# Two-block transformer step on one Trainium2 core: each expert weight unit of 1 MB asked for by two transfers of 512 KB

## The reference

```
# router: a group of 4, then the two best of its 8 experts; gates[n, e] is zero elsewhere
for e in range(N_EXPERTS):                               # 32
    hid = jax.nn.silu(t @ w_eg[e]) * (t @ w_eu[e])       # w_eg, w_eu: 1024 x 512
    out = out + gates[:, e:e + 1] * (hid @ w_ed[e])      # w_ed: 512 x 1024
```

## Time and profile before

| | |
|---|---|
| time, median of 3 runs | 1771.27 us |
| the profiled execution | 1775.45 us, its span 1773.4 us |
| granted TensorE clock, mean over the span | 0.995 of full speed |
| PE busy | 1745.6 us, 98% of the span |
| DVE, ACT, POOL busy | 954.2, 725.9, 42.0 us |
| HBM read | 426.70 MB, 241 GB/s over the span |
| `w_ed` units on line 338 | 64 of 1024 KB, median 18.5 us from issue to landing |
| `w_eg`, `w_eu` units into mring | 63 and 62 of 1024 KB, median 14.1 and 16.1 us |

### The profile page before, as it was taken

One profiled execution on the slowest core, in us unless ns is written; L12 is line 12 of the kernel. 1 busy time (PEld: TensorE's weight loads), 2 busy tenths in 40 slices (PEclk: granted clock), 3 DMA queues, 4 the chain that ended last, 5 costly groups with the idle time before them and its releaser, 6 DMA issues.

```text
span 1773.4 us, 24576 instructions
## 1 busy us (share of the span) xinstructions
PE 1745.6 (98%) x9801; PEld 1338.4 (75%) x9801; DVE 954.2 (54%) x1258; ACT 725.9 (41%) x1005; POOL 42.0 (2%) x57
## 2 busy tenths in 40 slices
PE   9999999999999999999999999999999999999998
PEld 8876454444445488888988888878888879888886
DVE  6684111111111286666787666676666864676665
ACT  5562111111111254346566434764346445554444
POOL 3000000000000000000000000000000001200000
PEclk9999999999999999999999999999999999999999
DMA  9278999999999855554435555365555544555552
GB/s 308 96 277 340 395 422 418 417 421 422 422 422 422 343 191 190 192 186 151 143 120 184 190 189 190 131 226 190 189 190 193 190 150 156 180 194 190 191 168 83
DMA packets 191242, 428.81 MB, mean 242 GB/s; under 512 B 7316, under 2 KB 145664, under 8 KB 166592
## 3 DMA queue, kind: packets, MB, share of 16 engines
q1 hardware_dynamic: 187952, 418.41, 64.7%
q0 software_dynamic: 3216, 9.37, 1.5%
HBM read 426.70 MB, written 1.05 MB: 241 GB/s over the span
## 4 chain that ended last, share of the span: by engine, by line
PE 89%; DVE 6%; ACT 3%; issue 1%; DMA 0%; DVEq 0%; ACTq 0%
PE pw L544 64%; PE acc L544 23%; DVE wl L1969 1%; PE pw L933 1%; ACT arena L1732 1%; DVE x L2431 0%; DMA raw<-in_odd_w_in 0%; ACT sm L1548 0%; ACT wh L1387 0%; DVE aa L1987 0%; DVE sm L2696 0%; DVE scr L2693 0%; PE pw L966 0%; PE pw L1315 0%; ACT arena L1710 0%
## 5 line engine op out<-in xcount | busy, mean ns | idle before, releaser
L544 PE MATMUL pw<-aa,wh 128*128 128x512 f32 (+1 forms) x2288 | 520.7, 354 | 0.7 <-ACTq L1800 0.4
L1969 DVE TENSOR_TENSOR wl<-raw,wh 128x2048 fp32r<-128x2048 f32 x204 | 460.9, 2297 | 95.4 <-ACT wh L1387 92.6
L544 PEld LDWEIGHTS pw<-aa,wh 128*128 128x128 f32 x2288 | 395.9, 190 | 54.5 <-issue 3.4
L1387 ACT ACTIVATE wh<-raw 128x2048 fp32r<-128x2048 f32 x204 | 380.0, 1907 | 40.3 <-DMA raw<-in_odd_w_in 23.2
L544 PE MATMUL acc<-wh,aa 128*128 128x512 f32 x1088 | 345.9, 391 | 0.4 <-DVE aa L2230 0.4
L544 PE MATMUL pw<-mring,arena 128*64 128x512 f32 x1512 | 333.9, 594 | 1.4 <-issue 1.3
L544 PE MATMUL pw<-aa,wl 128*128 128x256 f32 x1880 | 324.7, 283 | 0.0
L544 PEld LDWEIGHTS pw<-aa,wl 128*128 128x128 f32 x1880 | 281.4, 191 | 14.0
L544 PEld LDWEIGHTS pw<-mring,arena 128*64 128x64 f32 x1512 | 106.7, 137 | 202.5 <-issue 200.2
L544 PEld LDWEIGHTS acc<-wh,aa 128*128 128x128 f32 x1088 | 204.5, 188 | 43.0 <-DVE wl L1969 0.8
L544 PE MATMUL acc<-wl,aa 128*128 128x512 f32 x544 | 212.2, 390 | 0.0
(11 more groups left out here) (436 smaller groups left out, 1271.4 us busy)
## 6 DMA issues: line engine op xcount, KB each, us to landing
raw<-in_ffn_w_in SPq DMA_DIRECT2D x88, 1024.0 KB, 5.1
mring<-in_w_ed SPq DMA_DIRECT2D x64, 1024.0 KB, 18.5
mring<-in_w_eg SPq DMA_DIRECT2D x63, 1024.0 KB, 14.1
mring<-in_w_eu SPq DMA_DIRECT2D x62, 1024.0 KB, 16.1
raw<-in_ffn_w_out SPq DMA_DIRECT2D x44, 1024.0 KB, 5.0
raw<-in_odd_w_in SPq DMA_DIRECT2D x24, 1024.0 KB, 5.4
raw<-in_w_in SPq DMA_DIRECT2D x12, 1024.0 KB, 9.7
raw<-in_even_w_in SPq DMA_DIRECT2D x11, 1024.0 KB, 5.4
```

The costliest lines, as they stand in the source:

```text
L544: return pe.matmul(out, lhs, rhs, start=start, stop=stop, skip_group_check=True)
L1387: act.activation(wh[:, u % RING, :], raw[:, u % RING, :], ACT.Copy).then_inc(sig(f"{ep}_hi"), 1)
L1969: dve.tensor_tensor(wl[:, u % RING, :], raw[:, u % RING, :], wh[:, u % RING, :].bitcast(F32), ALU.subtract).then_inc(sig(f"{ep}_lo"), 1)
```

## The change

Each unit is now asked for by two transfers, issued one right after the other: the first half of the unit's rows (2 of 4, or 1 of 2, in every partition), then the second half. In a partition that is 4 KB each, one behind the other in HBM and in the slot. Each half adds 16 to the same semaphore as before, and PE waits for 32 where it waited for 16. Slots, order of units, waits of SP and places of PE's waits stay as they were. The two new lines in `expert_unit` move all later line numbers by 2.

```
-                sp.dma_start(dst, src).then_inc(sig(f"{landed}{n}"), 16)
+                rows_ = src.shape[1] // 2
+                for part in (slice(0, rows_), slice(rows_, 2 * rows_)):
+                    sp.dma_start(dst[:, part, :], src[:, part, :]).then_inc(sig(f"{landed}{n}"), 16)
...
                 if n not in held:
-                    pe.wait_ge(sig(f"m_landed{n}"), i * 16 + 16)
+                    pe.wait_ge(sig(f"m_landed{n}"), i * 32 + 32)
                 elif isinstance(i, int):
-                    pe.wait_ge(sig(f"e_landed{n}"), 16)
+                    pe.wait_ge(sig(f"e_landed{n}"), 32)
                 else:
-                    pe.wait_ge(sig(f"m_landed{n}"), i * 16)
+                    pe.wait_ge(sig(f"m_landed{n}"), i * 32)
...
-                pe.wait_ge(sig(f"{'m' if odd else 'e'}_landed{n}"), twos * 16 + 16)
+                pe.wait_ge(sig(f"{'m' if odd else 'e'}_landed{n}"), twos * 32 + 32)
```

## The result

The changed kernel takes 1784.59 us (median of 4 runs, 1783.35 to 1785.37) against 1770.9 us (median of 4 runs of the kernel before): 1.0067 times the time before, 95% interval 1.0055 to 1.0079. It is slower, by 10 to 14 us, and lies above the stated range. The forecast was 1773.5 us.

A forecast was written before the change was run, and what follows sets the result against it. The DMA stream was taken to bound the end of the expert stage. 17 + 3 = 20 ns a unit over 108 units, with 43 earlier ones absorbed, gave +2.2 us on 1771.27: 1773.5 us, range 1770.5 to 1780.5.

The forecast's parts named there:

- What bounds the kernel: Expert stage: PE lives on loads made ahead until used up; the stage ends with the DMA stream, 1.35 us recoverable at most.
- The price of the packets: Expert units as 4 KB instead of 8 KB packets: 17 ns more a unit, 20 ns with completions; ends 0 and 69 ns.
- My high end of 69 ns: Expert units: 8 more packets a unit at a fixed part of 8.6 ns, giving 9.3 us of delay.
- Completions and SP: Expert stage: doubled completions cost 0 to 19 ns a unit, 3 taken; SP's extra issues, 0.33 us each, cost nothing while covered.
- the cover: Transfers queued ahead while SP is held in an issue: 12 us instead of 25, enough to keep the DMA engines working.
- The count of units: Delay of the last pair's unit n=3: 108 late units count fully, 43 earlier ones only beyond 1.09 us of idleness.
- the dry stretch: DMA engines run dry at 302 to 320 us; this 1.09 us of idleness absorbs a slower stream before anything is delayed.
- The rule on small packets: Expert units: about 3 bus cycles of overhead a packet, an estimated 1.2% or 29 ns a unit, 3.4 us in sum.
- Dear packets: Rival, slower: every engine's stream from 318 us on, over 30 ns a unit, up to 1780.6 us; chance 0.36.
- Free packets: Rival, not slower: 8 KB and 4 KB packets stream alike, d near 0, 1769.9 to 1771.5 us; chance 0.18.
- a faster kernel: Rival: faster by over 0.2%, though no wait in the expert stage holds 3.5 us to give back; chance 0.04.
- A fixed part paid for each transfer: Rival: each added half of an expert unit pays 2.3 us, some 350 us in all, 2120 us; chance 0.02.

The follow-up runs named there:

- the contiguous megabyte: Against the kernel before: one transfer a unit with 4 KB packets, taken from a contiguous megabyte of HBM; 1783.72 us, ratio 1.0059.
- alternate partitions: Against the changed kernel: each unit's two transfers take the even and the odd partitions, with 8 KB packets; 1772.24 us, ratio 1.0001 to the kernel before.
- The late units: Against the changed kernel: only units of the second loop of loads (pairs 6 to 15) are split; 1782.53 us, ratio 1.0052 to the kernel before.
- The early ones: Against the changed kernel: only units up to pair 5 are split, later ones stay whole; 1777.7 us, ratio 1.0030 to the kernel before.

## Why the prediction was wrong

**What bounds the kernel: right.** PE's lead is used up by the DMA stream, nothing can come back, and every nanosecond of the unit ends on the time. The waits appeared at the place foretold, before the second half of a pair's first gate and up, and earlier than foretold. The second wait of a pair, for unit 1, was not foretold.

**The price of the packets: wrong, and this is the step that failed.** The prediction says: "I choose the value of the real 4 KB stream, 17 + 3 = 20 ns a unit." It measures 72 to 74 ns. The two ends that I subtracted came from different situations: 2.485 us from a queue that had run for long, 2.502 from transfers that ran alone. A stream that has just begun is some 2% faster with either packet. Where it starts anew behind its pause at 182 us, 8 KB packets run at 431 GB/s (before, 186 to 194 us) and 4 KB packets at 419 (after, 190 to 194):

```profile
DMA packets 471, 3.45 MB, mean 431 GB/s; under 512 B 50, under 2 KB 50, under 8 KB 50
```

```profile
DMA packets 457, 1.68 MB, mean 419 GB/s; under 512 B 48, under 2 KB 48, under 8 KB 457
```

From 198 to 206 us both have come down, to 421 and 410. In the same situation the step is thus 2.433 to 2.503 us, 70 ns, and the 431 stood in the trace that I had. The 418 GB/s of the earlier trace rows, which I took as a reason for "free", come from a window of 1.0 us with 51 packets, where one packet is 2%. A window of 1.53 us on the same stream (145.00 to 146.53 us) shows 428:

```profile
DMA packets 80, 0.66 MB, mean 428 GB/s; under 512 B 0, under 2 KB 0, under 8 KB 0
```

The line through 1 KB and 4 KB, both from lone transfers, gave a fixed part of 8.6 ns a packet; the runs show 9.0 to 9.4. My high end of 69 ns was thus nearly the answer, and I gave it 0.36 as the rival. Why the rate comes down by 2% soon after a stream has begun, with either packet, is open; the contiguous megabyte comes down to 410 as well.

**Completions and SP: right.** Both cost nothing measurable (alternate partitions, ratio 1.0001). Only the restart at 182 us loses something to the second transfers, 1.2 us by the window of 182 to 190 us, some 1.7 by the bytes. SP was held back at once, as foretold, and the cover held: the DMA row stays at 9 tenths.

**The count of units: wrong in its lesser part.** The formula gives 108 x 0.074 + 43 x 0.074 - 1.09 = 10.1 us for 74 ns, a time of 1781.4 us and so still too little; the stage grew by 12.86. The late units came out near it (7.3 against 8.0 by the stage). The early ones did not (3.9 against 2.1 to 2.5): I let the idle engines of 182.5 to 210.75 us absorb the slower packets, but that idleness lies at the restart, ahead of the units that it was to absorb, and the split made it longer. All 160 units from 182 us to unit 3 of the last pair cost 160 x 0.074 = 11.8 us; the loss of 1.2 to 1.7 at the restart and the 1.1 given back by the dry stretch about cancel. Some 0.5 to 1 us of 12.86 stays unexplained.

**The rule on small packets.** By the rule of the Trainium skill (DMA: Bandwidth & Descriptors, section Why small descriptors are slow (HBM only)) the estimate was 29 ns a unit. The runs show 72 to 74 ns, 2.5 times as much: a fixed cost per packet is there, and its size is the measured one. That the trace supports "about half" of the rule rested on the 17 ns and does not hold.

**The rivals.** Dear packets was the case; its price was a little over the 69 ns of its upper end. Free packets and a faster kernel did not occur. A fixed part paid for each transfer did not occur: the alternate partitions with twice the transfers are at 1.0001.

## What to carry to other kernels

Where a stage lives on loads made ahead, its waits say little about its margin: compare the time per unit of the stream with that of its user, and price every change of packet size by that. Cutting a transfer was free here when each partition's run kept its length and the pieces took alternate partitions; it cost by the packet when the run was cut, and far more when the pieces took neighbouring halves of the partitions. Take both sides of a difference from the same situation, and a window so long that one packet does not matter: a stream that has just begun does not stand for a queue that has run for long.

## What the runs showed of the hardware

Two transfers to neighbouring halves of the partitions, one behind the other in the queue, run at 264 GB/s, while two transfers to the 64 even and the 64 odd partitions run at 422, with packets of 8 KB in both. What is shared in the first case no run here shows.

SP's issues are held back when enough is queued, but the amount isn't a count of transfers, as I had supposed. At the end of the stage the longest time from issue to landing was 29.8 us before, about 12 transfers; 16.8 us after, about 13 transfers of half the size; 21.3 us with one transfer of 4 KB packets, about 8; and 22.8 us with alternate partitions, about 18. A larger packet, 16 KB, was not tried: it could give back at most the 1.35 us of the earlier trace rows.
